# First stage of a one-core layer kernel: ten tiles of x turned ahead of the first product, sums of squares later, four PSUM banks for the first four product tiles

## The reference

```
def _rmsnorm(x, g):
    ...
    y = xf * lax.rsqrt(jnp.mean(xf * xf, axis=-1, keepdims=True) + EPS)
    return (y * g.astype(jnp.float32)).astype(x.dtype)

def _in_proj(x, g_mix, w_in):
    B, T = x.shape[:2]
    z = _rmsnorm(x, g_mix) @ w_in
    cuts = np.cumsum([Q_COLS, 6 * KV_COLS, 3 * N_HEADS, SSM_WIDTH]).tolist()
    q, kv, gt, u, mg = jnp.split(z, cuts, axis=-1)
```

## Time and profile before

| | us |
|---|---|
| three runs | 2296.54, 2296.58, 2304.18; median 2296.58 |
| profiled execution, its own time | 2303.8 |
| its span, first to last record | 2302.0 |
| mean granted TensorE clock | 0.956 of full speed |
| busy: PE, PEld, DVE, ACT | 2123.1, 1979.0, 1087.4, 806.4 |
| first program, start to its last product | 0 to 247 |

### The profile page before, as it was taken

The page is one execution under the profiler, slowest core; times in us unless marked ns, Lnnn a source line. Parts: engine busy times, 40 slices in busy tenths (PEclk is TensorE's granted clock), DMA queues, the critical chain, the costliest instruction groups (busy, mean ns, idle before and its releaser), DMA issues.

```text
span 2302.0 us, 39034 instructions
## 1 busy us (share of the span) xinstructions
PE 2123.1 (92%) x15836; PEld 1979.0 (86%) x15836; DVE 1087.4 (47%) x1736; ACT 806.4 (35%) x1160; POOL 111.8 (5%) x166
## 2 busy tenths in 40 slices
PE   6999798898996799957999999999999999999997
PEld 5999788786896355537999989999999999999997
DVE  4343487843554255543555444444444444444443
ACT  4222232342342255544333333323332233233343
POOL 1000011000000112200000100000000000000011
PEclk8999899999996799978999999999999999999998
DMA  5745543443443988716555544455445554455543
GB/s 146 199 137 155 130 128 100 119 113 96 125 139 111 369 305 316 283 60 249 159 152 146 146 128 146 142 149 166 146 140 140 165 153 144 138 160 148 150 129 112
DMA packets 552675, 364.85 MB, mean 158 GB/s; under 512 B 64705, under 2 KB 528146, under 8 KB 551474
## 3 DMA queue, kind: packets, MB, share of 16 engines
q1 hardware_dynamic: 471042, 314.13, 44.2%
q10 hardware_dynamic: 80096, 41.25, 6.7%
q0 software_dynamic: 1424, 7.97, 0.9%
HBM read 345.58 MB, written 23.63 MB: 160 GB/s over the span
## 4 chain that ended last, share of the span: by engine, by line
PE 52%; ACT 1%; DMA 1%; DVE 1%; issue 0%; POOLq 0%; POOL 0%; SPq 0%; ACTq 0%
PE bank L279 52%; DMA w_raw<-in_w_attn_out_dram 1%; DVE w_lo L258 0%; ACT w_hi L253 0%; PE bank L2127 0%; ACT ysT L2155 0%; DVE rstd L2311 0%; ACT xT L2213 0%; ACT xT L2234 0%; DVE arena L2340 0%; ACT sq L2185 0%; PE bank L2136 0%; ACT hx L2160 0%; ACT oT L2213 0%; POOLq L147 0%
## 5 line engine op out<-in xcount | busy, mean ns | idle before, releaser
L279 PE MATMUL bank<-hx,w_hi 128*128 128x320 f32 x3328 | 734.3, 310 | 5.6 <-DVE w_lo L258 5.6
L258 DVE TENSOR_TENSOR w_lo<-w_raw,w_hi 128x2048 fp32r<-128x2048 f32 (+2 forms) x222 | 464.0, 2090 | 369.8 <-ACT w_hi L253 369.7
L279 PEld LDWEIGHTS bank<-hx,w_hi 128*128 128x128 f32 x3328 | 558.3, 188 | 6.1 <-DVE w_lo L258 6.1
L279 PE MATMUL bank<-hx,w_lo 128*128 128x320 f32 x1664 | 515.1, 310 | 0.0
L279 PE MATMUL bank<-act,w_hi 128*128 128x320 f32 x2176 | 485.1, 312 | 24.9 <-DVE w_lo L258 24.9
L253 ACT CAST w_hi<-w_raw 128x2048 fp32r<-128x2048 f32 (+2 forms) x222 | 385.8, 1738 | 334.5 <-PE bank L279 320.9
L279 PEld LDWEIGHTS bank<-act,w_hi 128*128 128x128 f32 x2176 | 368.1, 190 | 26.1 <-DVE w_lo L258 13.0
L279 PE MATMUL bank<-act,w_lo 128*128 128x320 f32 x1088 | 338.7, 311 | 0.0
L279 PEld LDWEIGHTS bank<-hx,w_lo 128*128 128x128 f32 x1664 | 313.2, 188 | 0.0
L655 PE MATMUL bank<-actr,half_hi 128*128 128x320 f32 x1024 | 240.5, 324 | 19.5 <-DVE half_lo L626 19.5
L279 PEld LDWEIGHTS bank<-act,w_lo 128*128 128x128 f32 x1088 | 206.6, 190 | 0.0
(11 more groups left out here) (388 smaller groups left out, 1900.5 us busy)
## 6 DMA issues: line engine op xcount, KB each, us to landing
arena<-in_cache_kv_dram SPq DMA_DIRECT2D x128, 512.0 KB, 7.1
w_raw<-in_w_gate_dram SPq DMA_DIRECT2D x44, 1024.0 KB, 5.1
w_raw<-in_w_up_dram SPq DMA_DIRECT2D x44, 1024.0 KB, 5.1
w_raw<-in_w_down_dram SPq DMA_DIRECT2D x64, 704.0 KB, 4.6
half_raw<-in_w_in_dram ACTq DMA_DIRECT2D x64, 512.0 KB, 4.2
w_raw<-in_w_in_dram SPq DMA_DIRECT2D x20, 1024.0 KB, 5.1
w_raw<-in_w_glu_dram SPq DMA_DIRECT2D x32, 512.0 KB, 4.6
w_raw<-in_w_out_dram SPq DMA_DIRECT2D x16, 1024.0 KB, 5.6
```

The source lines that it names most:

```text
L258: nc.vector.tensor_tensor(w_lo[s][:, 0:job.kt * job.width], raw[s][:, 0:job.kt * job.width], w_hi[s][:, 0:job.kt * job.width].bitcast(F32) ...
L279: mm = pe.matmul(bank[:, 0:NT], w[s][:, at:at + P], x[:, kk, :], start=first and k == 0 and m == 0, stop=final and k == job.kt - 1 and m == 2)
```

## The change

- PE turns ten slices ahead of the first product instead of four, and slice k + 10 between the slices of the product instead of k + 4.
- ACT rounds weight tile 0 behind turn 4 (before: behind turn 3) and weight tile 1 behind turn 11 (before: behind turn 13). The squares of the first half move from behind turn 7 to behind turn 15; weight tile 2 is rounded between the two halves' squares, weight tile 3 behind the square root. DVE follows the same order.
- Products 0 to 3 get banks 0 to 3 of their own. So PE no longer waits for the reads of products 0 and 1 before products 2 and 3, and the matmuls of the row of 1/rms move from in front of product 2 to behind it. DVE makes the rests of weight tiles 2 and 3 before it reads a product, not between the reads.

```diff
-        def multiply(pe, job, i, s, hi, lo, k0=0, each=None, last=None):
+        def multiply(pe, job, i, s, hi, lo, k0=0, each=None, last=None, own=None):
             pe.wait_ge(S(f"split_ready{s}"), i + (job.base + 2))
-            if not (job.joined and s):
+            if not (job.joined and s) and own is None:
 
                 pe.wait_ge(S(f"bank_free{s}"), i + (job.base + 1))
             for side in range(job.wide):
-                bank = PS[0 if job.joined else s + 2 * side]
+                bank = PS[0 if job.joined else own if own is not None else s + 2 * side]
...
-                for k in range(4):
+                AHEAD = 10
+                for k in range(AHEAD):
                     turn_x(k)
...
-                    if k + 4 < KT:
-                        turn_x(k + 4)
+                    if k + AHEAD < KT:
+                        turn_x(k + AHEAD)
                 mm.then_inc(S("tile_full0"), 1)
                 multiply(pe, job_q[0], 0, 1, actr[:, 0], actr[:, 1])
+                pe.wait_ge(S("gcol_copied"), 1)
+                multiply(pe, job_q[0], 1, 0, actr[:, 0], actr[:, 1], own=2)
                 pe.wait_ge(S("ones_ready"), 2)
                 pe.wait_ge(S("diag_ready"), 1)
...
                 mm.then_inc(S("rstd_full"), 1)
-                for s in range(2):
-                    multiply(pe, job_q[0], 1, s, actr[:, 0], actr[:, 1])
+                multiply(pe, job_q[0], 1, 1, actr[:, 0], actr[:, 1], own=3)
...
                 act.wait_ge(S("ones_ready"), 2)
-                turn(range(4))
+                turn(range(5))
                 round_tile(act, job_q[0], 0, 0)
-                turn(range(4, 8))
+                turn(range(5, 12))
+                round_tile(act, job_q[0], 0, 1)
+                turn(range(12, 16))
                 squares(0)
-                turn(range(8, 14))
-                round_tile(act, job_q[0], 0, 1)
-                turn(range(14, 16))
+                round_tile(act, job_q[0], 1, 0)
                 squares(1)
...
-                for s in range(2):
-                    round_tile(act, job_q[0], 1, s)
+                round_tile(act, job_q[0], 1, 1)
...
-                turn(range(4))
+                turn(range(5))
                 rest_tile(dve, job_q[0], 0, 0)
-                turn(range(4, 14))
+                turn(range(5, 12))
                 rest_tile(dve, job_q[0], 0, 1)
-                turn(range(14, 16))
+                turn(range(12, 16))
+                rest_tile(dve, job_q[0], 1, 0)
...
                 ins.then_inc(S("diag_ready"), 1)
+                rest_tile(dve, job_q[0], 1, 1)
                 dve.wait_ge(S("rstd_full"), 1)
...
-                first = scale_in(job_q[0], qT, 0, rstdq)
+                first = scale_in(job_q[0], qT, 0, rstdq, own=True)
                 first(0, 0)
-                rest_tile(dve, job_q[0], 1, 0)
                 first(0, 1)
-                rest_tile(dve, job_q[0], 1, 1)
                 first(1, 0)
```

More of the change, by code:

```diff
@@ L544, in _, with scale_in @@
                 dve.wait_ge(S("norm_order"), 3)
-                def scale_in(job, dst, t0, by):
+                def scale_in(job, dst, t0, by, own=False):
                     def read(i, s):
                         full(dve, job, i, s)
-                        V.tensor_tensor(dst[:, bass.ds(i * 2 + (t0 + s), 1), :].rearrange("p a n -> p (a n)"), PS[s][:, 0:NT],
+                        V.tensor_tensor(dst[:, bass.ds(i * 2 + (t0 + s), 1), :].rearrange("p a n -> p (a n)"), PS[2 * i + s if own else s][:, 0:NT],
                                         by, ALU.mult).then_inc(S(f"bank_free{s}"), 1)
```

## The result

The changed kernel takes 2290.45 us (median of 11 runs, 2280.5 to 2298.03), the kernel before, measured in the same sessions, 2303.93 us (11 runs, 2296.54 to 2311.56). The ratio is 0.9943, 95% interval 0.9922 to 0.9964: 13.5 us less, by the interval 8 to 18. The median of three runs that the prediction started from, 2296.58, was at the low end of what the kernel before does.

A forecast was written before the change was run, and what follows sets the result against it. PE bounds the kernel, so the term is product 3's end, 69.6 to 55.2: 14.4 less 0.4 for hand-overs, 14.0 us off the 2296.58 median gives 2283 us; range 2280 to 2293.

The forecast's parts named there:

- the second rival: Clock rises late (2285.9 us), or changed runs are of the long kind (2289.8), both together 2293.1; chance 0.28.
- The rival that the shorter executions have part of the gain already: Shorter runs lack the clock falls at 29.7 and 53.8, so the gain is 9.3 us: 2287.3; chance 0.2.
- What bounds: PE ends the program; behind product 3 it is busy 176.05 of 177.30 us, so all behind follows as a block.
- Start of product 0: Product 0 waits for turns 8 and 9, which need x's second half; it starts at 20.0, 2.6 us later.
- I take the first: In product 0 the clock rises after 5.46 us of pairs, not 13.6, so product 0 ends at 33.1.
- What turned it is that squares no longer stand among the turns: Product 0 ends at 33.1, before 40.84, because ACT's 3.42 us of squares no longer stand in front of turn 8.
- my lower bound of 10.7 for a late rise: Half clock for 13.6 us of product 0, which ends at 36.4, 3.3 us later; gain 10.7 us.
- The upper bound of 16.5: Full clock from the start of product 0, which then ends at 31; gain 16.5 us.
- the 0.4 for hand-overs: Taken off the 14.4 us sum for about eight hand-overs between engines in the first stage, 0.05 us each.
- Products 1 to 3: Product 1 33.1 to 40.1, product 2 to 47.2, product 3 48.1 to 55.2; stall of 3.7 us and clock fall gone.
- Slower: Clock stays at 1.2 GHz through the four products, ending 9.6 us later: 2306.2; decides beyond about 62 us; chance 0.03.
- the signs of being wrong: PE waits for w_lo before products 2, 3 or 4, product 0's slices wait for `h_ready`, or clock 0.50 beyond 35 us.

The follow-up runs named there:

- 16 ahead: The changed kernel with all sixteen turns ahead of product 0 instead of ten; 2291.07 us, ratio 0.9936 to the kernel before.
- bare first: The changed kernel with slices 0 to 7 of product 0 free of turns, turns 10 to 15 behind slices 7 to 12; 2286.98 us, ratio 0.9942 to before.
- the second trace of before: The kernel before, not edited, traced once more; 2305.49 us in one run.
- the squares back: The changed kernel with only the first half's squares moved back behind turn 7 on ACT; 2289.7 us, ratio 0.9953 to the kernel before.
- 4 ahead: The changed kernel with four turns ahead instead of ten, squares, roundings and banks as changed; 2290.89 us, ratio 0.9939 to the kernel before.

## Why the prediction was right, and where it was off

- **The size of the gain held**: 14.0 forecast, 13.5 measured. The absolute time did not, 2283 against 2290.45, for the base alone: three runs of the kernel before had a median of 2296.58, eleven have 2303.93. So 2290.45 lies where the second rival (chance 0.28) put it, at 2289.8 for executions of the long kind and 2293.1 for these with a late rise, and not at the forecast (0.45). The rival that the shorter executions have part of the gain already stays open: both traces of the kernel before are of executions of 2304 to 2305 us. What speaks against it is that the spread of 10 us lies behind the mark.
- **What bounds**: right. 177.30 and 177.32 us from product 3's read to the last product.
- **Start of product 0**: 20.0 forecast, 19.69 and 20.21 measured. It waits for the last of x, as said. The slack before the change was a little larger than written: PE turned slice 8 behind slice 4, at 24.44, not at 23.4.
- **Product 0**: the step that failed is "I take the first", the rise of the clock 5.5 us into product 0 while slices and turns alternate. It came at 32.5, 12.8 us in. In nine of the ten traces where pairs began at half clock (all but 16 ahead and bare first) they stayed there, 10.9 us in the changed kernel and 21.8 in the kernel before; the tenth is the trace that the prediction had. Three more pairs and two bare slices at half clock put product 0's end at 36.05, not 33.1, and with it the mark at 58.38, not 55.2. Full clock came 2 to 7 us behind the last turn in each of these nine (30.6 and 32.5 in the changed kernel, 39.3 and 46.2 in the second trace of before). The Trainium skill, page "TensorE: Matmul & The Clock Gate", part 4 (PE-mode transpose), has the rule that was weighed here: transposes do not count as PE-busy in the same way. These nine traces agree with it, and so do 3.60 us of turns alone at 0.50 and the eight bare slices in front, with full clock 4.9 us in; the first trace, with its rise 5.46 us into the pairs, does not. No run put matmuls of another kind in the place of the turns, so that it is the transposes which kept the clock down is argued, not shown.
- **The same trace misled on the squares**: "What turned it is that squares no longer stand among the turns" is wrong. At half clock ACT has the time for them between turns (no wait of PE among the pairs in the second trace nor with the squares back). The gain of product 0 comes from the turns: six fewer among its slices (6 x 1.02 us less, 2.3 of it given back by the later start), and the bare slices begin 9 us earlier (30.6 for 39.3 in the second trace of before, 39.6 with 4 ahead) and, behind them, full clock. Four ahead against ten measures it: 7.3 us by the first mark.
- **Why the sum was right all the same**: in part by luck. The early rise was taken for both kernels; it came in one of the four traces with four turns ahead and in neither of the changed kernel. Against the first trace the gain is 11.25, not 14.0 and near my lower bound of 10.7 for a late rise; but with a late rise, as in the other three, the mark of the kernel before lies 2.7 us later as well, and the gain is 13.4 (72.34 - 58.90). An error of 2.7 us in the one covered an error of 3.2 to 3.7 us in the other. The upper bound of 16.5 leaves out the 0.4 for hand-overs that the 14.0 and the 10.7 have; with it, it is 16.1.
- **Products 1 to 3**: right. No gap on PE, 7.04 and 7.05 us, no fall of the clock; the banks are worth 5.3 us by themselves (5.4 forecast as 3.7 + 1.7), 4.3 when they alone are taken out of the changed kernel. From the second trace of before the marks go 72.34, 67.00 with the banks, 65.67 with squares and roundings moved too, 58.90 with ten turns ahead: 5.3, 1.3 and 6.8. The middle step is within what product 0's start and the clock's rise vary by.
- **Slower**: full clock was there at 32.5 and 33.2 us in the changed kernel's traces and did not fall again in the first stage, far from the 62 at which that rival decides. Of the signs of being wrong none came: no wait in front of products 2, 3 and 4, no slice of product 0 that waits, no 0.50 in the column beyond 35 us in this stage.

## What to carry to other kernels

When small matmuls or transposes alternate with the products at the start of a kernel, look at the length of one slice in the timeline: if it stays at the half-clock length, every turn among the slices costs more (here 1.02 us for 0.62 at full clock, 1.06 less 0.44), and a stretch of bare products first can be worth more than an earlier start (16 ahead started 5.5 us later and had its mark 1.2 us earlier; eight bare slices first won 2.2 to 2.7 us). Put what PE can do while it waits in front (turns 4 to 7 cost nothing here), and enough bare slices ahead of the mixed ones.

A stall that stands in one trace may depend on the clock of that trace. Before a term of the sum rests on a clock event, take a second trace of the same kernel, and compare kernels by a mark in the stage that was changed when the rest of the program varies by more than the change.

## What the runs showed of the hardware

Pairs of slice and turn kept half clock for up to 21.8 us with PE busy without a gap, and in the bare-first order the same pairs held full clock once it was there (1.06 us, six in a row). Bare slices had half clock for 5.6 us and full clock behind that with 16 turns ahead, and for 4.9 us in the bare-first order. Until its first change the clock column reads 1.00, even where matmuls take the half-clock time (19.69 to 32.5 in the changed kernel), so the lengths of the rows decide there. The last part of x landed 6.0 to 7.3 us after its issue from one trace to the next, and with ten turns ahead this moved product 0's start between 19.69 and 20.54.
